# Expert items with the single group first, spread capacities, and recurrence gates between projection tiles

## The chip, the cores and the metric

The kernel runs on one core of one Trainium2 chip. The metric is the device time of the whole program in microseconds. TensorE (PE), VectorE (DVE), ScalarE (ACT), GpSimd (POOL) and SyncE (SP) each run their own instruction stream and meet at semaphores. All data is float32.

## The reference

Two models in a row, on 256 tokens of width 1024. The first block is a mixer of mLSTM and differential attention, followed by a mixture of 32 experts, of which each token takes four:

```python
top_val, top_idx = lax.top_k(logits, TOP_K)          # 4 of 32
gate = jax.nn.softmax(top_val, axis=-1)
hcat = xf[tok] @ w1[e] + b1[e]                       # 1024 -> 2048
act = h_glu * jax.nn.sigmoid(SWIGLU_ALPHA * h_glu) * (h_lin + 1)
y = act @ w2[e] + b2[e]                              # 1024 -> 1024
```

The second block has two layers on 272 tokens (16 of them meta tokens). Its first layer's mixer is a gated linear recurrence beside a sliding-window attention:

```python
r = sigmoid(blockwise(x, w_a) + b_a); i = sigmoid(blockwise(x, w_x) + b_x)
log_a = -LRU_C * r * softplus(-lam);  a = exp(log_a)
u = sqrt(-expm1(2 * log_a)) * (i * x)
h_t = a_t * h_(t-1) + u_t;            y_a = gelu(gate) * h
```

The attention in the first block takes the difference of two softmaxes: `a = p[:, :, 0] - lam * p[:, :, 1]`, of heads of 64 dimensions each.

## The kernel before

Weights stream through SP's queue in units of 1 MB ([128 partitions, 2048 columns]). Outside the expert stage they go through a ring of R = 6 slots; `project` multiplies one unit as two output tiles of 128 columns each, which ACT copies out of two PSUM banks in turn (`out_bank`, `tile_out`).

**The expert stage.** Tokens of an expert are gathered in groups of 32 (`GROUP`). The experts are sorted by load at run time, and place `j` of the order has room for `CAPACITY[j]` groups; a load above its capacity starts a loop behind the stage (`most > 0`). A place's groups are worked in items of at most two groups (`ITEMS`): for an item, PE multiplies the 8 units of the first matrix (`w1_step`, L2137, four column tiles of 32 rows for each group), and in the next round of the loop the 4 units of the second (`w2`, L2154). Between, ACT and DVE turn and activate the hidden values. Each of the 384 units (32 experts with 8 + 4) is loaded once into one of ES = 14 slots (8 spare places of the arena, and the ring), in the fixed order that the list `order` gives: the first matrix of the expert of item n, then the second matrix of that of item n - 1. The load number n (from 14 on) waits for release number n - 14, and releases come only from the last item of an expert (`released`, L758). After every 8 groups PE gathers the next chunk (`gather`, L2091), after every 4 it scatters results (`scatter`, L2106).

**mLSTM and attention.** In `m_rows` (L1945) PE spreads one of 4 gate rows over the partitions. In `d_scores` (L1996) it makes four score tiles of 128 x 512 for a head, two for each of the two maps; map m uses partitions 64 m to 64 m + 63 of q and k. DVE takes maxima and scales, ACT exponentials and copies; `phase` is a barrier of four engines.

**The recurrence.** PE makes the first two x tiles with `pre_unit`, six more and then eight gate tiles with `project`; after each second unit of the gates come four pairs of small matmuls, `lru_gates` (L2316). ACT copies the tiles, takes sigmoids, tanh, exponentials, one square root over everything (L1115), the GELUs, and only then copies K and V (L1123 and L1126), which PE's q tiles (L2343) wait for through the banks. DVE convolves x, computes 1/(1+tanh) and the products (`lru_input`), and after the square root multiplies, scans and multiplies by the gate for each of 8 tiles (`lru_scan`, L1692 to L1696). Then `swa_mask` (L1711) begins the sliding-window attention. POOL only clears two halves of kz here.

## Time and profile before

| | us |
|---|---|
| median of 3 runs | 2896.99 |
| lowest and highest | 2896.99, 2903.4 |
| the profiled execution | 2903.46 |
| its span, first to last instruction | 2901.6 |
| PE busy | 2517.1 (87%) |
| DVE busy | 768.3 (26%) |
| ACT busy | 552.0 (19%) |
| POOL busy | 16.3 (1%) |
| HBM read | 604.91 MB, 209 GB/s over the span |

A busy engine in the table is a mean over stages that have different limits. Lines such as L2137 are those of the kernel before. A timeline row is the start, the time that the group of like instructions takes, the engine, the line, the operation with output and inputs, and in brackets the idle time before it and what ended that.

### The profile page before, as it was taken

Reading aid. Unit: us, or ns where it says so; the run is one execution under the profiler, and the core shown is the slowest. Engines: PE = TensorE matmul, PEld = TensorE weight load, DVE = VectorE, ACT = ScalarE, POOL = GpSimd, SP = SyncE. Lnnn points to the kernel's source line nnn. Section 1 sums busy time; section 2 is a strip of 40 time slices with the busy share of each in tenths; the row PEclk is TensorE's granted clock in tenths of the full one; section 3 lists DMA queues with packets and bytes.
Section 4 is the critical chain, followed back from the end, with each engine's and each line's share of the span. In section 5 each row is a group of like instructions: output and inputs, shape, how many; then the busy total and the mean of one; then the engine's idle time right before and its main releaser. Section 6 shows DMA issues by size and latency. Waiting matters only on the chain. (4 is left out here: it accounts for less than half of the span.)

```text
span 2901.6 us, 36397 instructions
## 1 busy us (share of the span) xinstructions
PE 2517.1 (87%) x15176; PEld 1647.3 (57%) x15176; DVE 768.3 (26%) x1863; ACT 552.0 (19%) x1358; POOL 16.3 (1%) x25
## 2 busy tenths in 40 slices
PE   3999976779899898887868776989999999999998
PEld 1785743468634334332323223767887788667876
DVE  1010046621211111211101112670541325624421
ACT  2110111500212111111111112351211211412110
POOL 0000000000000000000000000000000000100000
PEclk7899997889799999989999897989999999999999
DMA  6222231025276999999999996313333334113432
GB/s 268 70 104 102 101 146 58 0 95 230 87 324 264 421 421 420 420 420 421 421 421 421 421 420 252 121 68 116 116 136 120 131 136 145 44 73 116 145 114 75
DMA packets 88101, 608.35 MB, mean 210 GB/s; under 512 B 10560, under 2 KB 12992, under 8 KB 17248
## 3 DMA queue, kind: packets, MB, share of 16 engines
q1 hardware_dynamic: 84752, 599.82, 52.2%
q10 hardware_dynamic: 3088, 5.78, 0.5%
q8 instruction: 122, 2.00, 0.3%
q0 software_dynamic: 96, 0.39, 0.0%
q14 instruction: 43, 0.35, 0.0%
HBM read 604.91 MB, written 1.05 MB: 209 GB/s over the span
## 5 line engine op out<-in xcount | busy, mean ns | idle before, releaser
L495 PE MATMUL bank<-arena,ring 128*128 128x272 f32 (+2 forms) x3456 | 826.1, 402 | 19.5 <-DVEq L559 18.4
L495 PEld LDWEIGHTS bank<-arena,ring 128*128 128x128 f32 x3456 | 658.9, 191 | 181.8 <-issue 45.9
L2137 PE MATMUL bank<-arena 128*32 128x512 f32 x2304 | 286.9, 620 | 50.1 <-DMA arena<-in_w_e 49.9
L521 PE MATMUL bank<-arena,ring 128*128 128x272 f32 x1216 | 287.7, 396 | 6.1 <-DVE arena L1640 6.1
L521 PEld LDWEIGHTS bank<-arena,ring 128*128 128x128 f32 x1216 | 233.0, 192 | 56.7 <-DVE arena L1640 7.0
L1516 DVE TENSOR_TENSOR arena<-bank,arena 128x256 f32<-128x256 f32 x56 | 23.8, 424 | 841.1 <-PE bank L2116 841.1
L2137 PE MATMUL bank<-ring,arena 128*32 128x512 f32 x1280 | 172.6, 654 | 41.4 <-DMA ring<-in_w_e 41.1
L2137 PEld LDWEIGHTS bank<-arena 128*32 128x32 f32 x2304 | 64.4, 111 | 216.4 <-DMA arena<-in_w_e 109.5
L2154 PE MATMUL bank<-arena 128*32 128x256 f32 x1760 | 118.8, 412 | 43.7 <-DMA arena<-in_w_e 39.7
L1626 DVE SCALAR_TENSOR_TENSOR arena<-arena,par 128x272 f32<-128x272 f32 x296 | 148.5, 502 | 10.5
L2154 PE MATMUL bank<-ring,arena 128*32 128x256 f32 x1824 | 115.0, 398 | 28.8 <-DMA ring<-in_w_e 25.5
L963 ACT ACTIVATE arena<-bank 32x256 f32<-32x256 f32 x224 | 84.0, 375 | 279.3 <-PE bank L2154 276.9
L2154 PEld LDWEIGHTS bank<-arena 128*32 128x32 f32 x1760 | 57.7, 116 | 109.0 <-DMA arena<-in_w_e 51.0
L2137 PEld LDWEIGHTS bank<-ring,arena 128*32 128x32 f32 x1280 | 34.2, 113 | 142.9 <-DMA ring<-in_w_e 93.1
L1624 DVE TENSOR_SCALAR arena<-arena,par 128x272 f32<-128x272 f32 x128 | 53.8, 421 | 215.4 <-ACT arena L1066 161.4
L507 PE MATMUL bank<-ring,arena 128*128 128x256 f32 x512 | 110.8, 379 | 0.0
L2154 PEld LDWEIGHTS bank<-ring,arena 128*32 128x32 f32 x1824 | 60.5, 113 | 88.1 <-DMA ring<-in_w_e 35.2
L507 PEld LDWEIGHTS bank<-ring,arena 128*128 128x128 f32 x512 | 97.3, 190 | 14.1 <-issue 1.0
L555 DVE RECIPROCAL arena<-arena 128x272 f32<-128x272 f32 x8 | 14.8, 1853 | 332.6 <-ACT arena L549 332.6
L977 ACT ACTIVATE arena<-bank 128x512 f32<-128x512 f32 x56 | 33.4, 597 | 287.4 <-PE bank L2137 287.4
L1066 ACT ACTIVATE arena<-bank 128x272 f32<-128x272 f32 x84 | 33.4, 398 | 266.2 <-PE bank L495 266.2
L1307 DVE TENSOR_SCALAR arena<-bank,acol 128x256 f32<-128x256 f32 x32 | 13.2, 477 | 202.8 <-PE bank L1945 202.8
(381 smaller groups left out, 2124.4 us busy)
## 6 DMA issues: line engine op xcount, KB each, us to landing
arena<-in_w_e SPq DMA_DIRECT2D x224, 1024.0 KB, 26.0
ring<-in_w_e SPq DMA_DIRECT2D x160, 1024.0 KB, 26.2
ring<-in_w_up SPq DMA_DIRECT2D x44, 1024.0 KB, 4.8
ring<-in_w_l SPq DMA_DIRECT2D x37, 1024.0 KB, 4.8
ring<-in_w_ada SPq DMA_DIRECT2D x24, 1024.0 KB, 6.2
ring<-in_w_proj SPq DMA_DIRECT2D x24, 1024.0 KB, 4.7
ring<-in_w_down SPq DMA_DIRECT2D x32, 704.0 KB, 4.0
ring<-in_w_merge SPq DMA_DIRECT2D x16, 1024.0 KB, 4.7
```

The source lines that it names most:

```text
L495: mm = pe.matmul(o[:, 0:n], ring[:, s, k * 256 + c * P:k * 256 + (c + 1) * P], rhs(k), start=(k == 0), stop=(k == KT - 1))
L507: mm = pe.matmul(o[:, 0:256], lhs(k, t), ring[:, s, k * 256:(k + 1) * 256], start=(k == 0), stop=(k == KT - 1))
L521: mm = pe.matmul(o[:, 0:n], ring[:, s, k * P:(k + 1) * P], rhs(part * kt + k), start=(part == 0 and k == 0), stop=(part == parts - 1 and k ...
L555: chain(dve.reciprocal(rs, rs))
L963: ins = act.activation(ys[j * GROUP:(j + 1) * GROUP, (g // QUAD) % 2, q * 256:(q + 1) * 256], bank[q * GROUP:(q + 1) * GROUP, 7, i * 256:( ...
L977: act.activation(ht[:, g % 2, :], bank[:, 4 + g % 2, :], ACT.Copy).then_inc(sem("ht_ready"), 1)
L1066: act.activation(up[:, j % 2, c, 2:], o[:, 0:L], ACT.Copy).then_inc(free, 1)
L1516: biased = step(dve.tensor_tensor(four(gate), four(bank[:, 6, 0:256]), bias(0, e), ALU.add))
L1624: chain(dve.tensor_scalar(dst, src[:, 0:L], w(0), b, ALU.mult, ALU.add))
L1626: ins = dve.scalar_tensor_tensor(out=dst, in0=src[:, k:k + L], scalar=w(k), in1=dst, op0=ALU.mult, op1=ALU.add)
L2137: mm = pe.matmul(bank[q * GROUP:(q + 1) * GROUP, 4 + g % 2, :], xe[:, (g // CHUNK) % 2, k, s:s + GROUP], w[:, q * 512:(q + 1) * 512], star ...
L2154: mm = pe.matmul(bank[q * GROUP:(q + 1) * GROUP, 7, i * 256:(i + 1) * 256], actT[:, n % 2, k, i * GROUP:(i + 1) * GROUP], w[:, c * D + q * ...
```

## The change

It does five things.

1. An expert with an odd number of groups starts with the item of one group; the pairs follow.
2. The capacities stay the same numbers in another order.
3. In the mLSTM, `m_rows` takes all 128 partitions of `crow`, which DVE clears ahead. In attention, q is copied by POOL into two tensors `qz`, each with the other map's 64 partitions zero, and the scores multiply all 128 partitions.
4. In the recurrence, the gate matmuls stand behind single tiles of the projections (`behind`); ACT takes the sigmoids there, copies K and V before the square root; DVE's softplus of lambda comes behind the convolutions.
5. The products x * i and gate * h go from DVE to POOL, with the semaphores `lru_gated` and `lru_scanned`.

```diff
-CAPACITY = [3, 1, 5, 1, 1, 4, 1, 1, 4, 1, 1, 3, 1, 3, 1] + [2, 1] * 8 + [1]
+CAPACITY = [3, 1, 2, 1, 3, 1, 2, 1, 4, 1, 2, 1, 1, 5, 1, 1, 2, 1, 4, 1, 2, 1, 3, 1, 2, 1, 2, 1, 1, 2, 1, 1]
...
-    for _g in range(0, _n, 2):
-        ITEMS.append((_at, list(range(STARTS[_at] + _g, STARTS[_at] + min(_g + 2, _n))), _g == 0, _g + 2 >= _n))
+    for _g in range(-(_n % 2), _n, 2):
+        ITEMS.append((_at, list(range(STARTS[_at] + max(_g, 0), STARTS[_at] + _g + 2)), _g <= 0, _g + 2 >= _n))
...
+                    if behind is not None:
+                        behind(2 * unit + c)
...
+        qz = [arena[:, a:a + NH_D * T].rearrange("p (a b) -> p a b", a=NH_D)
+              for a in (vm_at - 4 * 2 * T, vm_at + KT * T)]
...
+                if n >= 3:
+                    lru_sigmoids(n - 3)
+            def gate_tile(n):
+                o, free = tile_out(act, at, n % 2 == 1)
+                act.activation(ga[:, n, :], o[:, 0:L], ACT.Copy).then_inc(free, 1)
+
+            for n in range(3):
+                gate_tile(n)
+                lru_sigmoids(n + 5)
...
-            gate_tiles(2)
+            gate_tile(3)
             act.wait_ge(sem("lru_tanh"), 8)
             for n in range(8):
                 act.activation(rg[:, n, :], rg[:, n, :], ACT.Exp, scale=nlru[:, n:n + 1]).then_inc(sem("lru_decay"), 1)
-            gate_tiles(3)
-            act.wait_ge(sem("lru_ratio"), 8)
-            act.activation(th[:, :, :], th[:, :, :], ACT.Sqrt, scale=2.0).then_inc(sem("lru_root"), 1)
+            for n in range(4, 8):
+                gate_tile(n)
...
             act.activation(v0[0:META, 2, :], o[0:META, 2 * P:3 * P], ACT.Copy).then_inc(free, 1)
+            act.wait_ge(sem("lru_ratio"), 8)
+            act.activation(th[:, :, :], th[:, :, :], ACT.Sqrt, scale=2.0).then_inc(sem("lru_root"), 1)
...
+            chain(dve.memset(crow[:, :, :, :], 0.0))
...
-                dve.wait_ge(sem("xc_ready"), n + 1)
-                chain(dve.tensor_tensor(xc[:, n, :], xc[:, n, :], ig[:, n, :], ALU.mult))
 
             def lru_scan(n):
 
+                dve.wait_ge(sem("lru_gated"), n + 1)
                 chain(dve.tensor_tensor(xc[:, n, :], xc[:, n, :], th[:, n, :], ALU.mult))
-                chain(dve.tensor_tensor_scan(out=ig[:, n, :], data0=rg[:, n, :], data1=xc[:, n, :], initial=0.0,
-                                             op0=ALU.mult, op1=ALU.add))
-                dve.wait_ge(sem("lru_gelu"), n + 1)
-                dve.tensor_tensor(mix[:, n, :], ga[:, n, :], ig[:, n, :], ALU.mult).then_inc(sem("lru_mixed"), 1)
+                dve.tensor_tensor_scan(out=ig[:, n, :], data0=rg[:, n, :], data1=xc[:, n, :], initial=0.0,
+                                       op0=ALU.mult, op1=ALU.add).then_inc(sem("lru_scanned"), 1)
...
+            phase(pool, 1)
+            for m in range(2):
+                pool.memset(qz[m][64 * (1 - m):64 * (2 - m), :, :], 0.0)
+                pool.tensor_copy(qz[m][64 * m:64 * m + 64, :, :], qd[64 * m:64 * m + 64, :, :])
...
+            for n in range(8):
+                pool.wait_ge(sem("xc_ready"), n + 1)
+                pool.wait_ge(sem("lru_gate_read"), n + 1)
+                pool.tensor_tensor(xc[:, n, :], xc[:, n, :], ig[:, n, :], ALU.mult).then_inc(sem("lru_gated"), 1)
+            for n in range(8):
+                pool.wait_ge(sem("lru_scanned"), n + 1)
+                pool.wait_ge(sem("lru_gelu"), n + 1)
+                pool.tensor_tensor(mix[:, n, :], ga[:, n, :], ig[:, n, :], ALU.mult).then_inc(sem("lru_mixed"), 1)
...
-                pe.matmul(bank[:, 2 + i % 2, :], cst("ident", h, 1)[0:4, :].to_broadcast([4, P]), crow[0:4, d, :, :],
+                pe.matmul(bank[:, 2 + i % 2, :], cst("ident", h, 1).to_broadcast([P, P]), crow[:, d, :, :],
...
-                    pe.matmul(bank[:, j, :], qd[64 * m:64 * m + 64, h, qt * P:(qt + 1) * P],
-                              kd[64 * m:64 * m + 64, h, :], start=True, stop=True).then_inc(sem("scores"), 1)
+                    pe.matmul(bank[:, j, :], qz[m][:, h, qt * P:(qt + 1) * P], kd[:, h, :],
+                              start=True, stop=True).then_inc(sem("scores"), 1)
...
-            pre_unit()
-            project(pe, at, 3, ub_k, L, first=ub_first)
-            at.ub += KT
-            pe.wait_ge(sem("lru_loaded"), 16)
...
-            for half in range(2):
-                project(pe, at, 1, ub_k, L)
-                for n in range(4 * half, 4 * half + 4):
-                    lru_gates(n)
-            project(pe, at, 2, ub_k, L)
+            pre_unit()
+            pe.wait_ge(sem("lru_loaded"), 16)
+            project(pe, at, 3, ub_k, L, first=ub_first, behind=lambda c: lru_gates(c - 1) if c >= 1 else None)
+            at.ub += KT
+            project(pe, at, 4, ub_k, L, behind=lambda c: lru_gates(c + 5) if c < 3 else None)
```

## Rows read from the trace of the kernel before

**Rows 1.** GB/s of the page's 40 slices of 72.5 us

```profile
GB/s 268 70 104 102 101 146 58 0 95 230 87 324 264 421 421 420 420 420 421 421 421 421 421 420 252 121 68 116 116 136 120 131 136 145 44 73 116 145 114 75
```

**Rows 2.** windows: us, busy us of each engine, granted clock, DMA share, GB/s

```profile
783.00:815.00 32.00, 31.77 (x203) 16.49 (x206) 1.37 (x7) 4.87 (x7) 0.00 (x0) 0.86 0.03 6
...
877.00:902.00 25.00, 24.16 (x240) 14.56 (x236) 0.62 (x2) 5.80 (x13) 0.00 (x0) 1.00 0.05 7
...
902.00:1772.00 870.00, 710.95 (x6808) 276.37 (x6800) 123.82 (x427) 139.76 (x327) 0.00 (x0) 0.93 1.01 421
```

**Rows 3.** waits of SP's queue, 700 to 910: total us, times, longest

```profile
SPq L758 <- PE bank L2137: 89.6, 18, 37.4
```

**Rows 4.** timeline of PE, one of the paced steps: start, us, [idle before <- releaser]

```profile
1690.36 1.92 PE L2137 MATMUL bank<-arena 128*32 128x512 f32 x16 [0.58 <-DMA arena<-in_w_e]
```

**Rows 5.** timeline of PE, expert stage

```profile
797.96 15.72 PE L2137 MATMUL bank<-arena 128*32 128x512 f32 x144
...
834.59 3.64 PE L2154 MATMUL bank<-ring,arena 128*32 128x256 f32 x64
...
878.08 3.72 PE L2106 MATMUL bank<-arena 128*128 128x256 f32 x16
```

**Rows 6.** timeline of SP's queue, expert stage

```profile
900.09 1.19 SPq L758 DMA_DIRECT2D arena<-in_w_e  x2
```

**Rows 7.** timeline of PE, attention: scores (L1996) and values (L2014)

```profile
545.16 2.07 PE L1996 MATMUL bank<-arena 64*128 64x512 f32 x8
...
550.23 1.99 PE L2014 MATMUL bank<-arena 128*128 128x256 f32 x8 [0.69 <-ACT arena L899]
...
552.15 2.06 PE L1996 MATMUL bank<-arena 64*128 64x512 f32 x8
...
571.19 3.78 PE L2014 MATMUL bank<-arena 128*128 128x256 f32 x8 [0.69 <-ACT arena L899]
```

**Rows 8.** groups by form, PE, 100 to 350: count, busy us, mean ns

```profile
L495 PE MATMUL bank<-arena,ring 128*128 128x512 f32 x192 | 82.8, 593 | 0.0
```

**Rows 9.** timeline of PE, mLSTM: value matmuls

```profile
400.90 3.72 PE L1963 MATMUL bank<-arena 128*128 128x256 f32 x16 [0.92 <-DVE arena L1330]
...
414.14 6.70 PE L1963 MATMUL bank<-arena 128*128 128x256 f32 x16 [4.89 <-DVE small L1330]
```

**Rows 10.** timeline of POOL

```profile
742.87 1.80 POOL L1856 MEMSET arena<- 128x2048 f32 x1 [140.97 <-DVEq L559]
...
2505.03 0.77 POOL L1864 TENSOR_TENSOR arena<-arena 128x272 f32<-128x272 f32 x1 [2.26 <-DVE arena L1820]
```

**Rows 11.** timeline of DVE: around the second barrier, and beside POOL

```profile
483.74 0.42 DVE L1353 TENSOR_TENSOR arena<-arena,small 128x256 f32<-128x256 f32 x1
...
506.14 0.23 DVE L1368 TENSOR_TENSOR lamc<-par 128x1 f32<-128x1 f32 x2
...
2503.97 0.58 DVE L1814 TENSOR_TENSOR arena<-arena 128x416 f32<-128x416 f32 x1
...
2505.37 0.88 DVE L1814 TENSOR_TENSOR arena<-arena 128x416 f32<-128x416 f32 x1
```

**Rows 12.** timeline of all engines, recurrence

```profile
1885.28 2.02 ACT L1115 ACTIVATE arena<-arena 128x2176 f32<-128x2176 f32 x1 [9.15 <-DVE arena L1686]
...
1887.32 1.28 ACT L1119 ACT_TABLE_LOAD   x1
...
1889.50 0.43 DVE L1692 TENSOR_TENSOR arena<-arena 128x272 f32<-128x272 f32 x1
...
1891.09 0.43 DVE L1692 TENSOR_TENSOR arena<-arena 128x272 f32<-128x272 f32 x1
...
1892.10 6.91 PE L2343 MATMUL bank<-arena,ring 128*128 128x272 f32 x16 [8.62 <-ACT arena L1123]
...
1900.61 0.61 DVE L1711 SCALAR_TENSOR_TENSOR arena<-con,bank 128x384 f32<-128x384 f32 x1
...
1904.64 0.49 PE L2369 MATMUL bank<-con,arena 128*128 128x128 f32 x3
```

More of the change, by code:

```diff
@@ L484, in tile_taken, with project @@
             eng.wait_ge(sem(f"bank_read{b}"), n)
-        def project(pe, at, n_units, rhs, n, first=None):
+        def project(pe, at, n_units, rhs, n, first=None, behind=None):
             for unit in range(n_units):
@@ L1081, in _, with lru_sigmoids @@
             act.activation(lru1[:, :], lru1[:, :], ACT.Exp, scale=-1.0).then_inc(sem("lam_exps"), 1)
+            def lru_sigmoids(n):
+                act.wait_ge(sem("lru_gates"), n + 1)
+                b = 2 * (n % 2)
+                act.activation(rg[:, n, :], bank[:, b, 0:L], ACT.Sigmoid, bias=prm("lru_ba", n))
+                act.activation(ig[:, n, :], bank[:, b + 1, 0:L], ACT.Sigmoid, bias=prm("lru_bx", n))\
+                   .then_inc(sem("lru_gate_read"), 1)
             for n in range(8):
@@ L1087, in _ @@
                     act.activation(xr[:, n, 3:], o[:, 0:L], ACT.Copy).then_inc(free, 1)
-            def gate_tiles(unit):
-                for n in (2 * unit, 2 * unit + 1):
-                    o, free = tile_out(act, at, n % 2 == 1)
-                    act.activation(ga[:, n, :], o[:, 0:L], ACT.Copy).then_inc(free, 1)
-            def lru_sigmoids(n):
-                act.wait_ge(sem("lru_gates"), n + 1)
-                b = 2 * (n % 2)
-                act.activation(rg[:, n, :], bank[:, b, 0:L], ACT.Sigmoid, bias=prm("lru_ba", n))
-                act.activation(ig[:, n, :], bank[:, b + 1, 0:L], ACT.Sigmoid, bias=prm("lru_bx", n))\
-                   .then_inc(sem("lru_gate_read"), 1)
-            for unit in range(2):
-                gate_tiles(unit)
-                for n in range(4 * unit, 4 * unit + 4):
-                    lru_sigmoids(n)
+                if n >= 3:
[6 more added lines that the diff above has]
+                lru_sigmoids(n + 5)
             act.wait_ge(sem("lru_gate_read"), 8)
@@ L1679, in _ @@
                 tile_skip(at, n % 2 == 1)
+            dve.wait_ge(sem("lam_exps"), 1)
+            log1p(dve, chain, lru1[:, :], lru3[:, :], nlru[:, :])
+            chain(dve.tensor_scalar(lru2[:, :], prm("lru_lam", 0, 8), -1.0, 0.0, ALU.mult, ALU.max))
+            chain(dve.tensor_tensor(lru2[:, :], lru2[:, :], lru1[:, :], ALU.add))
+            chain(dve.tensor_scalar(lru2[:, :], lru2[:, :], LRU_C, None, ALU.mult))
+            dve.tensor_scalar(nlru[:, :], lru2[:, :], -1.0, None, ALU.mult).then_inc(sem("nlru_ready"), 1)
+            chain(dve.tensor_scalar(nsink[:, :], prm("sinks", 0, HEADS2 + 2), -1.0, None, ALU.mult))
             def lru_input(n):
@@ L1850, in _ @@
         def _(pool):
-            for n in range(1, 5):
+            phase(pool, 1)
+            for m in range(2):
+                pool.memset(qz[m][64 * (1 - m):64 * (2 - m), :, :], 0.0)
+                pool.tensor_copy(qz[m][64 * m:64 * m + 64, :, :], qd[64 * m:64 * m + 64, :, :])
+            for n in range(2, 5):
                 phase(pool, n)
```

12 lines of the change are left out of this document (3 added, 9 removed).

## The prediction, made before the change was run

> **What bounds the kernel now.** I read the page's 40 slices first. From slice 13 on the DMA engines move about 421 GB/s, eleven slices long; before that, in the expert stage's first slices, GB/s falls to 87, 324 and 264 [rows 1]. So the expert stage (some 780 to 1785 us) is paced by weight transfers, once they run. The windows make it exact: from 902 to 1772 us the queue moves 421 GB/s while PE is busy 711 of 870 us, so one 1 MB unit (1.0486 MB) takes 2.49 us, and in two holes, 783 to 815 and 877 to 902, almost nothing moves [rows 2]. The waits of SP's queue name the cause: 89.6 us of waiting on PE's first expert matmuls, that is, for a slot to come free [rows 3]. The holes, some 32 and 25 us, are time that the stage never gets back, since everything behind them is paced by transfers: where PE has a step, it starts it only when its unit lands [rows 4]. Outside this stage PE bounds most of the time; around the recurrence the chain alternates between DVE and ACT.
>
> **Part 1: single group first, capacities spread.** The capacities are the same multiset (56 groups, 39 items, 17 pairs), so neither the 384 units nor PE's matmuls change, and the overflow loop is entered for the same loads. What changes is when slots come free. There are 14 slots. An expert's first slot is released at the first step of its last item, so an expert of 5 groups keeps 12 slots through two whole items.
> First hole: PE starts the expert matmuls at 797.96; 144 instructions of 15.72 us are 18 group-steps (8 each), so 0.87 us per step of one group [rows 5]. Before, the first release needs 8 steps of the pair and one of the single, 17 group-steps, 14.8 us. After, 8 single steps and one pair step, 10 group-steps, 8.7 us. The first hole ends 6.1 us earlier.
> Second hole: with capacities 3, 1, 5 the third expert blocks the slots while PE works through two pairs; the next load is issued only at 900.09 [rows 6]. After, the third has 2 groups and the fourth 1, so no such hole forms there: 25 us saved. The expert of 5 now stands at the 14th place, inside the steady stretch, and there it makes a hole of its own. From the start of its first unit the queue has work for its 8 first-matrix units, the previous expert's 4 second-matrix units, its own 4 and 2 of the next: 18 x 2.49 = 45 us. PE needs, from that unit on: the single item at the transfers' pace, 12 x 2.49 = 30 us (its own matmuls are under that); then a pair's first matrix, 16 x 0.87 = 13.9; two hidden turns and the single's second matrix 3.6 [rows 5]; the first step of the last pair 1.7; about 2.3 from issue to first bytes, read off between 900.09 and 902 [rows 2, 6]. That is 52 us, and 3.7 more if a scatter falls there [rows 5]. So a hole of 7 to 11 us, and about 5 more when its second-matrix slots are held in the same way one item later: 13 in all, taken between 5 and 25. An expert of 4 (two pairs) releases after 30 + 1.7 us, under 45: no hole. The tail ends in experts of 2, 1, 1 as before.
> Sum of part 1: -6.1 - 25 + 13 = **-18 us**.
>
> **Part 2: attention scores and gate rows over all 128 rows.** A score matmul now multiplies 64 live and 64 zero rows. Before, the eight instructions of a head's four scores take 2.07 us [rows 7], while 192 instructions of the same 512 columns over 128 rows cost 431 ns each (82.8 / 192) [rows 8], 3.45 us for eight. So two of the four ran beside each other, one in each half of the array, and that ends: +1.4 us of PE per head. The Trainium skill, TensorE: Matmul & The Clock Gate, Part 3 (packing small matmuls), says that small-K matmuls in distinct row groups run concurrently; the trace agrees, and this edit gives that up. Is it on the path? The head's period is 6.99 us (545.16 to the next scores at 552.15 [rows 7]) and is set by DVE and ACT. PE's own loop becomes 2.0 (values) + 3.45 + 1.05 (turns) + 0.7 (ACT's copy) = 7.2: +0.2 per head, 8 heads, +1.5. Against it, PE is idle less, and its clock fell in this stage: the same eight value matmuls take 1.99 us at 2.4 GHz and 3.78 at 1.2 GHz after idling [rows 7]. I take 0 for attention, +2 to -4 as bounds at a high clock. The gate rows (4 live rows, now 128) keep their time; in the mLSTM loop the 16 value matmuls take 3.72 us, and 6.70 where PE had idled 4.89 us [rows 9]. Three such places give back at most 6.6 us if fuller matmuls held the clock; the idle time that precedes them stays, so I take -1. The added clears and copies of q stand on POOL between two barriers. A clear of 2048 columns takes 1.80 us; POOL's multiply of 272 columns takes 0.77 [rows 10], so a copy of 2048 is under 5.8: at most 15.2 us together, and DVE needs from its last step before the barrier (484.2) to 506.4 in that place [rows 11]. Hidden; if a copy cost over 9 us it would show. One DVE clear more in the gate stage stands beside projections: 0.
>
> **Part 3: recurrence.** Three moves. (a) The gate matmuls go between projection tiles, so PE doesn't wait for ACT's sigmoids (about 1 us). (b) ACT copies K and V out before the square root. Before, PE idles 8.62 us to 1892.10 for that copy, then runs a q tile in 6.91 us, at 1.2 GHz [rows 12]. That idle goes. But what is late next is DVE: its mask at 1900.61 waits for the scans, and those for the root. The root (2.02, plus a table load of 1.28) now stands behind the V copy; V ends at 1892.10 - 8.62 = 1883.5, about 1.4 less with (a), so the root ends at 1886 instead of 1887.3. (c) DVE's scan loop gives the second multiply to POOL. A period is 1.59 us before [rows 12] and 1.16 without the 0.43 of a multiply; over 8, -3.4. However both engines then read two operands from SBUF at once. The row bears on that: a DVE multiply of 416 columns takes 0.58 us alone and 0.88 while POOL's multiply (0.77) runs [rows 10, 11]. With POOL's 0.77 falling between each DVE multiply and scan, I put a period at 1.75, between 1.16 and 1.16 + 0.77, and the loop at 1.3 us longer than before. The Trainium skill, SBUF — State Buffer, "Who interferes with whom", calls the shared port an exclusive lock, held for the whole instruction, against a DVE instruction with two SBUF inputs; by it the period would be 1.93, and the 0.88 agrees in kind. So the mask comes at 1900.4, where it was. And PE, which before had just run a q tile when the first probabilities came (1904.64 [rows 12]), has by then done two q tiles and idled some 10 us, after which I expect 1.2 GHz: its q tile of 6.91 us shows some 7 us of such work, in which 3.5 are lost, now inside the PE-bound loop of 6.6 us. Part 3: **+3 us** (-5 if ports don't collide and the clock holds; +4). POOL's first multiplies wait for gates that are long read; nothing that is queued behind them is due before the next phase.
>
> **Sum.** -18 + 0 - 1 + 3 = -16 us. The profiled execution took 2903.5 us (span 2901.6 and 1.9 around it), the median of three runs is 2897.0, 6.5 lower. I carry the difference over: 2897 - 16 = **2881 us**. About 0.3%, 8.7 us, is what a measurement of this kernel can tell from no change.
>
> **Rivals.**
> A, no hole at the expert of 5: if PE is far enough ahead there, all of 31 us is won, 2868. Against it is that PE cannot be ahead of the transfers.
> B, the hole is as large as before: 25, and -6 remains: 2893, within 0.3%. For it: the same 12 slots, the same two further items.
> C, the fuller matmuls hold TensorE's clock in mLSTM and attention: another -8: 2873. For it, both places fall after idle time; against, the idle time before the mLSTM ones isn't touched.
> D, ports don't collide and the clock survives in part 3: -5 in place of +3: 2873.
> E, slower: the array stays at 1.2 GHz through attention, where the scores are now serial. A head would be 3.8 (values) + 6.9 + 2.0 + 0.7 = 13.4 against 7.2 on average, over seven heads +43: 2881 + 43 = 2924. It decides from the point where PE's loop at the low clock exceeds DVE's 7 us. Against it: PE would then be busy 95% of the time, and at 545 and 550 us a less busy PE ran at 2.4 GHz [rows 7].
> F, that the change doesn't do what it says (a capacity that a load exceeds) would start the overflow loop; the sorted capacities are the same, so I give it nothing.
>
> **How the numbers follow.** Chances: forecast 0.48, A 0.09, B 0.13, C 0.13, D 0.12, E 0.05. Forecast, A, C and D are faster by over 8.7 us: 0.82 and, with the edge of B, 0.84; within 0.3%: 0.12; slower: 0.04. The range leaves out E and the far ends of A and B: 2864 to 2893.
>
> **What would show it.** Right: in the windows after the change, transfers resume near 809, run without a hole past 900, and pause 8 to 15 us near 1200; the last expert's work ends 18 us earlier. The score group takes about 3.5 us a head, head periods stay near 7. PE's q tile follows V's tile at once, and the mask starts within 2 us of where it does, counted from the start of the projections. Wrong: a hole at 870 to 900 that stays, head periods over 8 us, or POOL's copies ending after DVE's part of that phase.

## The result

The changed kernel takes 2872.64 us (median of 4 runs, 2872.32 to 2876.0) against 2897.26 us (2896.99 to 2903.4): a ratio of 0.9913, with a 95% interval of 0.9895 to 0.993. The prediction was 2881 us in a range of 2864 to 2893. The sign and the largest term were right, and the gain was 8 us larger than forecast. Two of the smaller terms were wrong, as the sections below show. The 2872.64 us lie at the 2873 us of the rivals C and D and not at the forecast.

The span of the profiled execution is 2870.6 us, against 2901.6 before. Windows of the expert stage after; columns as in [rows 2]:

```profile
783.00:811.00 28.00, 28.00 (x226) 11.78 (x228) 2.01 (x6) 5.28 (x8) 0.00 (x0) 0.96 0.40 152
811.00:1170.00 359.00, 307.35 (x2993) 124.04 (x2986) 54.86 (x190) 61.94 (x145) 0.00 (x0) 0.92 1.01 418
1170.00:1230.00 60.00, 58.81 (x613) 25.98 (x615) 8.83 (x30) 12.56 (x29) 0.00 (x0) 1.00 0.78 310
```

The run of transfers now reaches from 811 to 1170 us at 418 GB/s; the gap of 877 to 902 us [rows 2] is gone, and one smaller gap stands at 1170 to 1230, where 310 GB/s instead of 421 are 60 x (1 - 310/421) = 15.8 us lost. SP's issues there show why; two units are issued at 1181.45, and then none for 20 us:

```profile
1181.45 1.50 SPq L763 DMA_DIRECT2D arena<-in_w_e  x2
1202.04 2.05 SPq L763 DMA_DIRECT2D ring<-in_w_e  x2
...
1210.86 2.05 SPq L763 DMA_DIRECT2D ring<-in_w_e  x2
1218.09 2.05 SPq L763 DMA_DIRECT2D arena<-in_w_e  x2
```

**Where the gain is.** To see what belongs to an edit and what to an execution, I took the time between fixed instructions in every profiled execution; each row of this table is such a stretch in us.

| stretch | before | after | after, second execution | same code elsewhere |
|---|---|---|---|---|
| mLSTM: first row sums (L1966, L1983) to the 28 sums behind the loop (L1974, L1991) | 101.35 | 98.46 | 97.92 | 97.9 to 98.5 with the change, 100.7 to 101.4 without |
| the lambda matmul (L1988, L2005) to the first merge matmul (L495) | 93.96 | 90.39 | 90.34 | 90.4 with, 93.0 and 94.0 without |
| expert stage: first expert matmul to DVE's residual add (L1587, L1594) | 990.60 | 974.31 | 974.92 | 974.2 to 975.7 with, 990.5 without |
| recurrence: first projection (L495) to the out-projection (L521, L523) | 148.57 | 144.66 | 145.74 | 143.6 to 145.7 with, 148.4 without |
| merge to the first expert matmul | 197.48 | 196.12 | 196.08 | 195.6 to 197.5, in both codes |
| residual add to the first projection | 25.45 | 23.09 | 25.38 | 23.0 to 25.5, in both codes |
| start to the first row sums | 363.33 | 362.96 | 360.76 | 361.0 to 363.2, in both codes |
| the 28 sums to the lambda matmul | 41.83 | 41.60 | 41.52 | 41.5 to 41.6 with, 41.8 and 40.2 without |
| out-projection to the end | 939.05 | 939.04 | 938.47 | 937.0 to 941.1, in both codes |

In the first four stretches every execution with the change in question is shorter than every one without it: -16.3 (part 1), -2.9 and -3.6 (part 2), -3.9 (part 3), together -26.7 us between these two profiles. The experiments below, which undo one part at a time, give 16.2, 4.9 and 3.8 us for the same stretches. Part 2 is the least certain: without it the 28 sums to the lambda matmul took 40.2 us once, 1.4 less than with it, so that from the first row sums to the merge it is worth 3.5 us by that experiment and 6.7 by the comparison of before and after. The merge and the norm stretch, 3.7 us of the 31.0 between the two spans, change with the execution, and so do the start and the end. The medians give -24.6 in the first comparison and -26.3 in the second (2871.63 against 2897.89).

### The profile page after: what moved, and what is told of

Its sections match the earlier page's. It is cut to its first block and busy times, and to the rows that moved or that the text cites. A ratio compares the mean times of both kernels' runs of the same rounds, so it can differ in the third digit from the quotient of the medians.

```text
span 2870.6 us, 36400 instructions
## 1 busy us (share of the span) xinstructions
PE 2506.2 (87%) x15176; PEld 1645.5 (57%) x15176; DVE 766.7 (27%) x1846; ACT 550.9 (19%) x1358; POOL 36.5 (1%) x45
## 5 line engine op out<-in xcount | busy, mean ns | idle before, releaser
L495 PE MATMUL bank<-arena,ring 128*128 128x272 f32 (+2 forms) x3456 | 827.0, 402 | 19.5 <-DVEq L561 18.4
L495 PEld LDWEIGHTS bank<-arena,ring 128*128 128x128 f32 x3456 | 658.7, 191 | 181.8 <-issue 46.0
L2154 PE MATMUL bank<-arena 128*32 128x512 f32 x2112 | 271.2, 636 | 50.6 <-DMA arena<-in_w_e 50.6
L523 PE MATMUL bank<-arena,ring 128*128 128x272 f32 x1216 | 287.7, 396 | 6.1 <-DVE arena L1647 6.1
L523 PEld LDWEIGHTS bank<-arena,ring 128*128 128x128 f32 x1216 | 233.0, 192 | 56.7 <-DVE arena L1647 7.0
L2154 PE MATMUL bank<-ring,arena 128*32 128x512 f32 x1472 | 187.9, 628 | 49.5 <-DMA ring<-in_w_e 49.5
L2171 PE MATMUL bank<-arena 128*32 128x256 f32 x1984 | 127.4, 402 | 26.9 <-DMA arena<-in_w_e 24.2
L2154 PEld LDWEIGHTS bank<-ring,arena 128*32 128x32 f32 x1472 | 40.2, 111 | 158.3 <-DMA ring<-in_w_e 93.9
L2171 PE MATMUL bank<-ring,arena 128*32 128x256 f32 x1600 | 103.3, 406 | 20.7 <-DMA ring<-in_w_e 16.0
L2171 PEld LDWEIGHTS bank<-ring,arena 128*32 128x32 f32 x1600 | 53.0, 115 | 74.4 <-issue 25.5
L1071 ACT ACTIVATE arena<-bank 128x272 f32<-128x272 f32 x84 | 33.4, 397 | 266.3 <-PE bank L495 266.3
L1057 ACT ACTIVATE arena<-bank 128x272 f32<-128x272 f32 x32 | 12.7, 397 | 282.6 <-PE bank L523 282.6
```

The source lines that it names most:

```text
L495: mm = pe.matmul(o[:, 0:n], ring[:, s, k * 256 + c * P:k * 256 + (c + 1) * P], rhs(k), start=(k == 0), stop=(k == KT - 1))
L523: mm = pe.matmul(o[:, 0:n], ring[:, s, k * P:(k + 1) * P], rhs(part * kt + k), start=(part == 0 and k == 0), stop=(part == parts - 1 and k ...
L1071: act.activation(up[:, j % 2, c, 2:], o[:, 0:L], ACT.Copy).then_inc(free, 1)
L2154: mm = pe.matmul(bank[q * GROUP:(q + 1) * GROUP, 4 + g % 2, :], xe[:, (g // CHUNK) % 2, k, s:s + GROUP], w[:, q * 512:(q + 1) * 512], star ...
L2171: mm = pe.matmul(bank[q * GROUP:(q + 1) * GROUP, 7, i * 256:(i + 1) * 256], actT[:, n % 2, k, i * GROUP:(i + 1) * GROUP], w[:, c * D + q * ...
```

## The experiments

In all of them the times of before were taken on the same chip: 2897.55 us for the first four, 2895.18 for the next four, 2897.89 for the last three. A median of four runs scatters by some 3 us, so for terms of a few us I go by the stretches.

### Part 1 undone

```diff
-CAPACITY = [3, 1, 2, 1, 3, 1, 2, 1, 4, 1, 2, 1, 1, 5, 1, 1, 2, 1, 4, 1, 2, 1, 3, 1, 2, 1, 2, 1, 1, 2, 1, 1]
+CAPACITY = [3, 1, 5, 1, 1, 4, 1, 1, 4, 1, 1, 3, 1, 3, 1] + [2, 1] * 8 + [1]
...
-    for _g in range(-(_n % 2), _n, 2):
...
+    for _g in range(0, _n, 2):
...
```

> The changed kernel with part 1 undone: old capacities, pairs first; parts 2 and 3 stay. Theory (slots held until an expert's last item): in the two traces the expert stage, from the first expert transfer to the end of its last step, takes 17.6 us less after the change, so this one gives 2872.6 + 17.6 = 2890 us, first release about 14.8 us after the first expert matmul, and the pause of the transfers of some 25 us before the third expert's slots come free is back. Rival (the stage gained because of what the other parts do to TensorE's clock): the pause is back but the time stays under 2880.

Measured: 2886.8 us, ratio 0.9954 (0.9937 to 0.9971). The expert stage takes 990.52 us, as before the change (990.60); the first release comes 15.06 us after the first expert matmul (9.06 with the change), and by windows of 5 us some 27.7 us of transfers are lost between 860 and 895 us. So part 1 is worth 16.2 us of this stretch and needs no help from the others; the medians differ by 14.2. The 17.6 that I expected contained 1.3 us from ahead of the first expert matmul, which is a matter of the execution.

### Single first alone, in the kernel before

```diff
-    for _g in range(0, _n, 2):
-        ITEMS.append((_at, list(range(STARTS[_at] + _g, STARTS[_at] + min(_g + 2, _n))), _g == 0, _g + 2 >= _n))
+    for _g in range(-(_n % 2), _n, 2):
+        ITEMS.append((_at, list(range(STARTS[_at] + max(_g, 0), STARTS[_at] + _g + 2)), _g <= 0, _g + 2 >= _n))
```

> The kernel before with nothing but the single group first; old capacities (3, 1, 5, ...). Theory: the second pause ends when the last item of the expert of 5 begins. Ahead of that step PE now has 7 groups of the first matrix and 5 of the second instead of 8 and 6, at 6.9 and 3.6 us a group, less 0.9 because the step itself is of a pair: the pause ends 9.7 us earlier, and the 6.1 us of the first pause are inside that, not on top. 2897.3 - 9.7 = 2887.6 us. Rival 1 (the two pauses are separate sums, only the first shrinks): -6.1, 2891. Rival 2 (the order within an expert doesn't matter): 2897.

Measured: 2893.15 us, ratio 0.9976 (0.9964 to 0.9989); the expert stage 986.39 us, 4.2 less than before. The interval of the time, -3.2 to -10.4 us, holds both rival 1's -6.1 and my -9.7 and decides nothing; the stage says that it was less than either. SP's issues from the end of the second pause, in this kernel and behind it in the kernel before:

```profile
891.90 2.05 SPq L758 DMA_DIRECT2D arena<-in_w_e  x2
896.07 2.05 SPq L758 DMA_DIRECT2D ring<-in_w_e  x2
900.23 5.48 SPq L758 DMA_DIRECT2D arena<-in_w_e  x4
913.14 1.22 SPq L758 DMA_DIRECT2D ring<-in_w_e  x2
```

```profile
902.54 1.19 SPq L758 DMA_DIRECT2D ring<-in_w_e  x2
904.98 2.91 SPq L758 DMA_DIRECT2D arena<-in_w_e  x4
915.32 1.22 SPq L758 DMA_DIRECT2D ring<-in_w_e  x2
```

Counted from the first expert matmul (797.41 and 797.96), the pause ends after 94.5 us instead of 102.1, 7.6 us earlier, which is near the 9.7 of the account. But then the last item is a pair: a slot comes free every 2.1 us, as each step has two groups' work (two units each at 891.90, 896.07, 900.23), where before one came free in 1.2 (two from 900.09 [rows 6], two from 902.54, four from 904.98). The next slots, of the expert behind it, come at 913.14, 115.7 us after the first matmul, against 915.32 and 117.4: 1.6 us earlier. By then PE has multiplied all five groups by the first matrix, in either order. So the order within an expert sets when its first slots come; what comes behind them is set by the whole expert's work, and 4.2 us remain at the end of the stage. My account had stopped at the first release.

### Pairs first, in the changed kernel

```diff
-    for _g in range(-(_n % 2), _n, 2):
-        ITEMS.append((_at, list(range(STARTS[_at] + max(_g, 0), STARTS[_at] + _g + 2)), _g <= 0, _g + 2 >= _n))
+    for _g in range(0, _n, 2):
+        ITEMS.append((_at, list(range(STARTS[_at] + _g, STARTS[_at] + min(_g + 2, _n))), _g == 0, _g + 2 >= _n))
```

> The changed kernel with its new capacities, but pairs first as before. Theory: the first release comes 6.1 us later, and at the expert of 5 a pair's second matrix (7.1 us) stands ahead of the release instead of a single's (3.6), with a single's step (0.9) instead of a pair's (1.7): 2.7 us more pause there, perhaps twice. 2872.6 + 6.1 + 2.7 to 5.4 = 2881 to 2884 us. Rival (all of part 1's gain is that the expert of 5 stands later): 2873.

Measured: 2873.93 us, ratio 0.9909 (0.9892 to 0.9926), which by the times alone can't be told from the changed kernel's. The expert stage is 977.76 us, 3.45 more. The first release is 6.0 us later (15.07 after the first matmul), as the account says. The pause at the expert of 5 got shorter, not longer: from 1165 to 1225 us the mean is 327 GB/s, 60 x (1 - 327/421) = 13.4 us lost instead of 15.8:

```profile
1165.00:1225.00 60.00, 54.25 (x598) 22.15 (x598) 9.68 (x32) 9.52 (x22) 0.00 (x0) 0.97 0.80 327
```

The reason lies in the same point. PE can't be ahead of the transfers, so the expert's first item runs at their pace; with a pair there, three groups are left behind it instead of four. So 12.8 of the 16.2 us of part 1 (990.52 to 977.76) are the new order of the capacities; the order within an expert brings 3.5, which is 6.0 at the start less 2.4 here.

### The expert of 5 as pair, single, pair

```diff
-    for _g in range(-(_n % 2), _n, 2):
-        ITEMS.append((_at, list(range(STARTS[_at] + max(_g, 0), STARTS[_at] + _g + 2)), _g <= 0, _g + 2 >= _n))
+    _split = {5: [2, 1, 2]}.get(_n, [1] * (_n % 2) + [2] * (_n // 2))
+    for _i, _w in enumerate(_split):
+        _g = STARTS[_at] + sum(_split[:_i])
+        ITEMS.append((_at, list(range(_g, _g + _w)), _i == 0, _i == len(_split) - 1))
```

> The changed kernel, the expert of 5 groups worked as pair, single, pair instead of single, pair, pair. Its first item runs at the pace of the transfers (30 us for 12 units) whether it has one group or two (a pair needs 21 us), so the larger one should be there. Theory: ahead of the release stand a single's first matrix (6.9 instead of 13.9) and a pair's second (7.1 instead of 3.6): 3.4 us less pause at the first matrix and about as much or more at the second, since one group less (10.5 us) is left behind the first item. 2872.6 - 3.4 to -10 = 2863 to 2869 us, and a pause near 1200 us that is shorter by as much. Rival (the pause is set by all five groups' work): 2872.6.

Measured: 2867.14 us, ratio 0.9891 (0.9874 to 0.9907); the expert stage 970.32 us, 4.0 less.

```profile
1165.00:1225.00 60.00, 54.09 (x574) 21.66 (x570) 11.18 (x37) 11.43 (x27) 0.00 (x0) 0.97 0.85 340
```

60 x (1 - 340/421) = 11.5 us are lost at the pause instead of 15.8. The single group first pays at the very start, where everything is loaded and PE is late (6.0 us); at the expert of 5, inside the paced stretch, the larger item belongs first. For the experts of 3 this was not tried by itself.

### Part 2 undone

```diff
-                pe.matmul(bank[:, 2 + i % 2, :], cst("ident", h, 1).to_broadcast([P, P]), crow[:, d, :, :],
+                pe.matmul(bank[:, 2 + i % 2, :], cst("ident", h, 1)[0:4, :].to_broadcast([4, P]), crow[0:4, d, :, :],
...
-                    pe.matmul(bank[:, j, :], qz[m][:, h, qt * P:(qt + 1) * P], kd[:, h, :],
-                              start=True, stop=True).then_inc(sem("scores"), 1)
+                    pe.matmul(bank[:, j, :], qd[64 * m:64 * m + 64, h, qt * P:(qt + 1) * P],
+                              kd[64 * m:64 * m + 64, h, :], start=True, stop=True).then_inc(sem("scores"), 1)
```

(and the clears and copies left out)

> The changed kernel with part 2 undone: gate rows from 4 partitions, scores from 64, no clears and copies of q. Theory of the forecast: mLSTM + 1, attention 0: 2873.6 us; score groups 2.07 us again, head period 6.99. Theory from the trace after (fuller matmuls held the clock): mLSTM's end came 3.3 us earlier after the change and attention's last values another 1.3: 2872.6 + 4.8 = 2877.4 us, with some heads at 1.2 GHz (values 3.78 us) before the last. Rival (which heads run at 1.2 GHz differs from execution to execution whatever the matmuls): 2873, low heads or not.

Measured: 2874.65 us, ratio 0.9931 (0.9915 to 0.9948). The median, 2.0 us above the changed kernel's, hardly speaks. The stretches: mLSTM 100.72 us (98.46 with the change, 101.35 before), lambda matmul to merge 93.02 (90.39, 93.96), but between these two 40.2 (41.6, 41.8). Timeline rows of PE at these places, in this kernel and then in the changed one:

```profile
363.97 1.12 PE L1957 MATMUL bank<-arena,con 4*128 4x512 f32 x2
...
384.91 5.15 PE L1975 MATMUL bank<-arena 128*128 128x256 f32 x16 [4.89 <-DVE small L1336]
...
412.73 6.58 PE L1975 MATMUL bank<-arena 128*128 128x256 f32 x16 [4.89 <-DVE small L1336]
...
483.90 5.15 PE L1991 MATMUL bank<-arena,con 128*128 128x256 f32 x16 [3.57 <-ACT arena L539]
...
517.96 3.47 PE L2026 MATMUL bank<-arena 128*128 128x256 f32 x8 [0.69 <-ACT arena L904]
...
572.42 5.26 PE L2032 MATMUL bank<-arena,con 128*128 128x256 f32 x16 [1.15 <-ACT arena L539]
```

```profile
364.68 1.02 PE L1962 MATMUL bank<-arena,con 128*128 128x512 f32 x2
...
385.34 5.38 PE L1980 MATMUL bank<-arena 128*128 128x256 f32 x16 [4.89 <-DVE small L1337]
...
413.01 5.38 PE L1980 MATMUL bank<-arena 128*128 128x256 f32 x16 [4.89 <-DVE small L1337]
...
482.45 6.52 PE L1996 MATMUL bank<-arena,con 128*128 128x256 f32 x16 [3.57 <-ACT arena L539]
...
516.68 1.99 PE L2031 MATMUL bank<-arena 128*128 128x256 f32 x8 [0.69 <-ACT arena L904]
518.51 3.60 PE L2013 MATMUL bank<-arena 128*128 128x512 f32 x8
...
525.55 3.60 PE L2013 MATMUL bank<-arena 128*128 128x512 f32 x8
...
571.29 3.69 PE L2037 MATMUL bank<-arena,con 128*128 128x256 f32 x16 [1.15 <-ACT arena L539]
```

Two things are in the mLSTM's stretch. Two gate rows take 1.02 us over 128 rows and 1.12 over 4. With the matmuls just ahead of them, which end 0.1 us sooner as well, that is 0.19 us a time and 1.1 us over the six times in the stretch. The rest is TensorE's clock. Three groups of 16 value matmuls stand behind 4.89 us of idle time; 3.72 us is what such a group takes at 2.4 GHz throughout (at 400.90 [rows 9]). They took:

| | first | second | third |
|---|---|---|---|
| without full rows, 3 executions | 5.15 to 5.37 | 6.58 to 6.70 | 5.38 to 5.68 |
| with full rows, 10 executions | 5.24 to 5.38 | 5.12 to 5.38 | 5.07 to 5.29 |

Only the second differs by over a microsecond in each of them, and at the next place it goes the other way: the 16 sums behind 3.57 us of idle time take 5.15 us in this kernel, 6.43 to 6.55 with full rows, and 6.74 in the kernel before. So behind the same idle time the same matmuls came out short in one place and long in another, in either kernel. That full rows bring the clock back sooner in the mLSTM is not shown; where a group falls in time is a rival that stands.

In attention the sign is the same in all of them. The first values take 1.99 us in all ten executions with full scores and 3.47 to 3.78 in the three without, the 16 sums at the end 3.69 against 5.26 to 5.92, and the stretch to the merge 90.3 to 90.4 against 93.0 to 94.0. The granted clock agrees: 0.82 and 1.00 from 505 to 515 and 515 to 525 us in the changed kernel, 0.50 and 0.70 in this one. Whether the reason is the rows themselves, the longer busy time of the scores (3.60 us against 2.06) or, again, where the stage falls in time was not tried.

### Part 3 undone

The changed kernel with the recurrence of the kernel before (items 4 and 5 of the change backwards); its core:

```diff
-            project(pe, at, 3, ub_k, L, first=ub_first, behind=lambda c: lru_gates(c - 1) if c >= 1 else None)
+            project(pe, at, 3, ub_k, L, first=ub_first)
...
+            for half in range(2):
+                project(pe, at, 1, ub_k, L)
+                for n in range(4 * half, 4 * half + 4):
+                    lru_gates(n)
```

> The changed kernel with part 3 undone: gate matmuls in two blocks, root ahead of the K and V copies, all products on DVE; parts 1 and 2 stay. Forecast: part 3 costs 3 us, so 2869.6. Theory from the trace after: from the first projection matmul of the recurrence to the steady q tiles it gained 2.0 us, so 2874.6. Rival: two more differences belong to it, 2.4 us less in the norm ahead of the projections and 1.8 us less behind the last q tile, both at 1.2 GHz in the trace before: 2878.8. If those were chance, they show here in any case or in none.

Measured: 2875.79 us, ratio 0.9929 (0.9912 to 0.9946). From the first projection to the out-projection 148.45 us (144.66 with the change). So part 3 gains 3.8 us where I had put a loss of 3; against the second execution of the changed kernel (145.74) it is 2.7. The two other differences that I named are not part 3's: the norm's 25.4 us came back in the second execution of the changed kernel.

### The gate product back on DVE

```diff
-                dve.tensor_tensor_scan(out=ig[:, n, :], data0=rg[:, n, :], data1=xc[:, n, :], initial=0.0,
-                                       op0=ALU.mult, op1=ALU.add).then_inc(sem("lru_scanned"), 1)
+                chain(dve.tensor_tensor_scan(out=ig[:, n, :], data0=rg[:, n, :], data1=xc[:, n, :], initial=0.0,
+                                             op0=ALU.mult, op1=ALU.add))
+                dve.wait_ge(sem("lru_gelu"), n + 1)
+                dve.tensor_tensor(mix[:, n, :], ga[:, n, :], ig[:, n, :], ALU.mult).then_inc(sem("lru_mixed"), 1)
```

> The changed kernel with the product gate * h back on DVE (x * i stays on POOL). Theory: DVE and POOL share their way to SBUF; a scan takes 1.17 us beside POOL's product and 0.72 alone. Here the scans are 0.72 again, the period is 0.44 + 0.72 + 0.43 = 1.59 instead of 1.53, and the mask starts 0.5 us later: 2873. Rival (the scan took 1.17 for another reason): scans of 1.17 and a period of 1.96, 3.4 us later: 2876.

Measured: 2876.0 us, ratio 0.9928 (0.9912 to 0.9945). One period, here and in the changed kernel (DVE, then POOL):

```profile
1863.84 0.43 DVE L1698 TENSOR_TENSOR arena<-arena 128x272 f32<-128x272 f32 x1
1864.31 0.72 DVE L1699 TENSOR_TENSOR_SCAN arena<-arena 128x272 f32<-128x272 f32 x1
...
1865.43 0.43 DVE L1698 TENSOR_TENSOR arena<-arena 128x272 f32<-128x272 f32 x1
```

```profile
1859.91 0.42 DVE L1698 TENSOR_TENSOR arena<-arena 128x272 f32<-128x272 f32 x1
1860.37 1.17 DVE L1699 TENSOR_TENSOR_SCAN arena<-arena 128x272 f32<-128x272 f32 x1
1861.45 0.41 DVE L1698 TENSOR_TENSOR arena<-arena 128x272 f32<-128x272 f32 x1
...
1860.08 0.87 POOL L1877 TENSOR_TENSOR arena<-arena 128x272 f32<-128x272 f32 x1 [30.82 <-DVE arena L1699]
1861.61 0.87 POOL L1877 TENSOR_TENSOR arena<-arena 128x272 f32<-128x272 f32 x1 [0.66 <-DVE arena L1699]
```

The scan is 0.72 us again and the period 1.59, against 1.17 and 1.53. From the first scan to the mask it is 12.22 us against 11.37: 0.85 more, 0.5 for the eight periods and 0.4 for the last product, which on POOL nobody waits for. The profiled execution was the slowest of the four, and the rest of its 6.9 us over the changed kernel's lies where the code is the same: the norm took 24.66 us (23.09), the matmuls ahead of the experts 1.3 more, and the part behind the recurrence 1.9 more. The medians differ by 3.4 us; that those are such differences too is not shown.

### The root ahead of the K and V copies

```diff
+            act.wait_ge(sem("lru_ratio"), 8)
+            act.activation(th[:, :, :], th[:, :, :], ACT.Sqrt, scale=2.0).then_inc(sem("lru_root"), 1)
             act.wait_ge(sem("bank_read0"), at.out // 2)
...
             act.activation(v0[0:META, 2, :], o[0:META, 2 * P:3 * P], ACT.Copy).then_inc(free, 1)
-            act.wait_ge(sem("lru_ratio"), 8)
-            act.activation(th[:, :, :], th[:, :, :], ACT.Sqrt, scale=2.0).then_inc(sem("lru_root"), 1)
```

> The changed kernel with the square root back ahead of the GELUs and of the K and V copies; the rest of part 3 stays. Theory: the start of the attention is set by DVE's mask, which waits for the scans, which wait for the root. DVE's last ratio is ready at 1849.8, so the root ends near 1852 instead of 1858.8, scans end near 1864, and the mask starts 6.6 us earlier than in the changed kernel, at 1864: 2866. V is copied near 1857, so the first q tile comes 2 us later and is hidden. Rival (PE's idle time ahead of its first q tile sets it to 1.2 GHz as before the change, which eats 3.5 us): 2869.5. Rival 2 (K and V copies are what mattered): 2875.

Measured: 2865.61 us, ratio 0.9899 (0.9883 to 0.9916). ACT's root, DVE's first product and mask, and PE's first q tile and first turn:

```profile
1849.39 2.02 ACT L1121 ACTIVATE arena<-arena 128x2176 f32<-128x2176 f32 x1 [2.32 <-DVE arena L1693]
...
1851.44 0.44 DVE L1698 TENSOR_TENSOR arena<-arena 128x272 f32<-128x272 f32 x1 [2.08 <-ACT arena L1121]
...
1863.39 0.58 DVE L1715 SCALAR_TENSOR_TENSOR arena<-con,bank 128x384 f32<-128x384 f32 x1
...
1856.21 3.90 PE L2356 MATMUL bank<-arena,ring 128*128 128x272 f32 x16 [1.79 <-ACT arena L1129]
...
1867.21 0.55 PE L2382 MATMUL bank<-con,arena 128*128 128x128 f32 x3 [1.30 <-DVE arena L1733]
```

From the first projection to the mask it is 76.9 us, against 83.7 in the changed kernel: 6.8 us, all of it kept to the end (7.0 by the medians). V is copied at 1856.09. PE's idle time ahead of the q tile is 1.79 us, and the tile takes 3.90 us, at 2.4 GHz, so the first rival is out; ahead of the first turn 1.30 us are left of 9.93. So part 3 without this one move would gain 10.7 us instead of 3.9. The mask, as the prediction said, is what is late, and moving the root behind the copies held it back.

### The changed kernel again, and two better ones

The changed kernel once more; the changed kernel with both edits of above (pair, single, pair and the early root); and the same with the root in two instructions:

```diff
+            for n, (a, z) in enumerate(((0, 6), (6, 8))):
+                act.wait_ge(sem("lru_ratio"), z)
+                act.activation(th[:, a:z, :], th[:, a:z, :], ACT.Sqrt, scale=2.0).then_inc(sem("lru_root"), 1)
...
-            dve.wait_ge(sem("lru_root"), 1)
...
             for n in range(8):
+                dve.wait_ge(sem("lru_root"), 1 if n < 6 else 2)
                 lru_scan(n)
```

> The changed kernel once more, to see which stretches of two executions of the same code differ. Theory: the stretches that gained beyond their instructions in the first comparison (from the end of the expert stage to the first projection 25.5 to 23.1 us, from the first expert transfer to the first expert matmul 98.1 to 96.8) belong to executions and not to the edits: here they may show either value, while the expert stage from first to last step (974.3), the stretch from the step between the mixers to the merge (90.4) and the one from the first projection of the recurrence to the mask (83.7) come out within 0.3 us. Median 2872. Rival (they are effects of the edits): 23.1 and 96.8 again.

> The changed kernel with both improvements: the expert of 5 worked as pair, single, pair, and the square root ahead of the GELUs and the K and V copies. Theory: the two stand in different stages and add up: 4.0 us of the expert stage and 6.8 of the recurrence, by the two traces. 2872 - 10.8 = 2861 us. Rival (part of the gain of either was chance of its executions): 2865 to 2868.

> The same with the square root in two instructions, tiles 0 to 5 and 6 to 7, so that the first part runs beside DVE's last two ratios. Theory: the scans start when DVE's ratios end (2.1 us earlier than with one root), the mask would follow 2.1 us earlier, but it needs PE's first scores, which end about 0.7 us after that point: mask 1.4 us earlier, 2859.6 us. Rival (PE's q tile, due after the V copy, is now what is late, and a shorter idle time doesn't count): the same time as with one root, 2861.

Measured: 2871.63 us (0.9908, 0.9891 to 0.9924), 2861.31 (0.9873, 0.9857 to 0.989) and 2858.51 (0.9867, 0.9851 to 0.9884). The second execution of the changed kernel shows what differs without an edit: its norm stretch is 25.38 us, as before the change, with the same code as the one that took 23.09. The stretch from the first expert transfer to the first expert matmul stayed low here (96.8 us), but was 98.1 in the kernel with the gate product on DVE, whose code there is the changed kernel's. The stages of the change repeated, the expert stage to 0.6 us, not to 0.3. Both edits add up (10.3 us of the 10.8). With the root in two, the first projection to the mask takes 74.8 us instead of 76.9: the whole 2.1, not 1.4, since V's copy and so the scores come 1.4 us earlier too. How DVE's and POOL's products meet shows here too (DVE's products and scans from the first on, then POOL's):

```profile
1844.33 0.43 DVE L1701 TENSOR_TENSOR arena<-arena 128x272 f32<-128x272 f32 x1
1844.80 0.73 DVE L1702 TENSOR_TENSOR_SCAN arena<-arena 128x272 f32<-128x272 f32 x1
1845.44 0.42 DVE L1701 TENSOR_TENSOR arena<-arena 128x272 f32<-128x272 f32 x1
...
1847.62 0.94 DVE L1701 TENSOR_TENSOR arena<-arena 128x272 f32<-128x272 f32 x1
1848.60 1.17 DVE L1702 TENSOR_TENSOR_SCAN arena<-arena 128x272 f32<-128x272 f32 x1
1849.69 0.93 DVE L1701 TENSOR_TENSOR arena<-arena 128x272 f32<-128x272 f32 x1
...
1846.98 4.25 POOL L1880 TENSOR_TENSOR arena<-arena 128x272 f32<-128x272 f32 x4 [23.12 <-ACT arena L1128]
```

While POOL has no product, because the GELUs aren't there, a period is 1.09 us (1845.44 to 1846.53); once it catches up on four products in a row, DVE's multiply takes 0.94, its scan 1.17 and a period 2.07 (1847.62 to 1849.69).

## Why the prediction was right, and where it wasn't

**Part 1, -18 predicted, -16.3 measured.** The first hole: 6.1 us predicted, 6.0 measured (15.06 to 9.06 us from the first expert matmul to the first release). The second hole of 25 us (27.1 by windows of 5 us) is gone. The hole at the expert of 5: 7 to 11 and about 5 behind it were worked out and 13 taken; by windows of 5 us, 10.8 are lost from 1190 to 1210 and 5.0 behind that, 15.8 in all. The 3.7 us for a scatter, priced and left out of the sum, fell there too: PE's scatter at 1212.31 (3.72 us) stands between SP's issues at 1210.86 and 1218.09. A place that the sum lacked, gathers and a scatter near 1030 us, lost 2.3. So rival A (no hole) and rival B (as large as before) are out. The reason given was right for the first-matrix slots, but the prediction held the single group first to be a gain everywhere, and at this expert it costs 4.0 us against a pair, since the first item's work is hidden whatever it is.

**Part 2, attention 0 predicted, -3.6 measured (-2.6 by the experiment); mLSTM -1, -2.9 measured (-2.3).** The instructions came out as costed: scores 3.60 us (3.45), a head's period 7.04 (7.2), POOL's copies 1.88 and 1.89 us (under 5.8) and hidden from 481.0 to 488.4. By the Trainium skill, TensorE: Matmul & The Clock Gate, Part 3 (packing small matmuls), small matmuls in different row groups run at the same time, which this edit gives up; the 2.06 and 3.60 us agree with it. The stage got shorter all the same. Two steps failed. One is "The gate rows (4 live rows, now 128) keep their time": they take 1.02 us instead of 1.12, and that is 1.1 of the mLSTM's 2.9 us. The other is the 0 for attention and the -1 for the clock in the mLSTM, "the idle time that precedes them stays, so I take -1". The idle time did stay (4.89 us); of the three places one is unchanged (5.37 and 5.38 us), one went from 6.70 to 5.38 and one from 5.68 to 5.24, 1.8 us in all. These 1.8 are near the -1 and, by the sums behind the loop, need not be the edit's; the 0 for attention is the larger miss. Rival C named a clock that is held, with 8 us more for it; from the first row sums to the merge the two profiles give 5.7 more than the -1, the experiment 2.5 more. The bounds (+2 to -4, and 6.6 at most) held both. Rival E (1.2 GHz through attention) is out: from 516.68 us on all values take 1.99 until the last. Why attention's clock was higher stays open.

**Part 3, +3 predicted, -3.9 measured (-2.8 with the second execution of the changed kernel).** This is the step with the wrong sign. Timeline rows of the changed kernel, ACT's V copy and root, DVE's first product and mask, and PE from the first q tile on:

```profile
1854.91 0.38 ACT L1130 ACTIVATE arena<-bank 128x256 f32<-128x256 f32 x1 [3.97 <-PE bank L2346]
...
1856.75 2.02 ACT L1133 ACTIVATE arena<-arena 128x2176 f32<-128x2176 f32 x1
...
1858.80 0.44 DVE L1698 TENSOR_TENSOR arena<-arena 128x272 f32<-128x272 f32 x1 [8.99 <-ACT arena L1133]
...
1870.64 0.58 DVE L1715 SCALAR_TENSOR_TENSOR arena<-con,bank 128x384 f32<-128x384 f32 x1
...
1854.80 3.93 PE L2356 MATMUL bank<-arena,ring 128*128 128x272 f32 x16
...
1874.45 0.90 PE L2382 MATMUL bank<-con,arena 128*128 128x128 f32 x3 [9.93 <-DVE arena L1733]
1875.15 1.65 PE L2370 MATMUL bank<-arena 128*128 128x128 f32 x4
1876.59 0.85 PE L2382 MATMUL bank<-con,arena 128*128 128x128 f32 x3
1877.23 0.91 PE L2370 MATMUL bank<-arena 128*128 128x128 f32 x4
1877.97 3.83 PE L2356 MATMUL bank<-arena,ring 128*128 128x272 f32 x16
```

Taken in order. The V copy and q tile come at once, as said. The root ends 71.8 us after the first projection, before 73.3 (1887.30 [rows 12] less 1814.01): 1.5 earlier, 1.3 predicted. The scans take 11.8 us, 1.53 a period, where 1.75 was predicted: that is 1.8 us. The estimate between 1.16 and 1.93 leaned on the 0.88 of a multiply beside POOL [rows 10, 11]; in fact only the scan is held up, by 0.45, and the multiply ahead of it runs beside POOL's product at 0.41. By the Trainium skill, SBUF — State Buffer, "Who interferes with whom", the port that VectorE and GpSimd share is an exclusive lock. The scan agrees: it ends 0.6 us behind POOL's product, about its own length alone. The period of 1.93 that I took from it doesn't come, because I counted POOL's product as behind the multiply: the multiply starts first, at 1861.45 against POOL's 1861.61, and isn't delayed. Where POOL's products stand back to back, in the kernel with two roots, both are delayed and the period is 2.07. The last product of 0.4 is off the path too, which the sum forgot. Then PE: it idled 9.93 us, as predicted (10), and was at 1.2 GHz behind it, as predicted (granted clock 0.50 from 1874 to 1877 us). But the low rows (0.90, 1.65 and 0.85 us) end at 1877.23, 2.8 us on; the next scores (0.91) and the q tile (3.83) are at 2.4 GHz (0.97 from 1877 to 1885). I had put 7 us of such work and 3.5 lost, from the one q tile of 6.91 [rows 12]. From the mask to the first steady q tile (1913.73 before, 1884.61 after) it is 13.12 before and 13.97 after: 0.85 lost. So the mask was put 2.7 us too late and the clock's loss 2.7 too high; what is left, up to 1.9 us behind the steady q tiles, differs between executions of the changed code (from the mask to the out-projection 59.9 to 62.0 us; 61.8 to 62.0 with the old recurrence). Rival D had the sign (-5), but neither of its conditions held as stated: the clock fell, for 2.8 us only, and DVE's scan did meet POOL's product.

**The sum.** By the two profiles the errors are 5.5 us in part 2 and 6.9 in part 3, both in one direction, and part 1 was put 1.7 too high: the four stretches give 26.7 us where 16 were predicted. By the experiments, with part 2 at its 3.5 us, it is 23.5. The time lay in the range because the range was wide enough for rivals C and D: the bounds of the unknown costs (-4 in attention, -6.6 in the mLSTM loop, -5 in the recurrence) reached as far as the errors did. C and D together had been given 0.25, and the forecast's own sums for parts 2 and 3 did not hold; that the errors stayed inside the range is in part luck.

## What to carry to other kernels

When buffers are released only at an item's end and transfers set the pace, try the largest work unit first in a group, since it runs under the transfers (4.0 us here, for one group of five), and the smallest first where everything is already loaded and the compute engine is late. Before moving a copy ahead of an operation on ACT, ask which of the two the last-arriving engine waits for: here the early copies only gave PE 10 us of idle time, and the early root gave the whole kernel 6.8 us. And compare several executions by stretches between fixed instructions before explaining a difference of 3 us: several stretches here differed by 1.3 to 2.4 us between executions of the same code, and the long one at the end by 4.

## What was unexpected of the hardware

- In attention TensorE was at 2.4 GHz earlier with scores over all 128 rows, slower in themselves (3.60 us against 2.06): the first values took 1.99 us in ten executions of ten, and 3.47 to 3.78 in three of three without. In the mLSTM the same 16 matmuls behind the same 4.89 us of idle time took between 5.07 and 6.70 us, in one and the same execution 5.37, 6.70 and 5.68.
- Two matmuls of 512 columns over 128 rows, between others over 128 rows, took 1.02 us; over 4 rows 1.12.
- A DVE multiply of 272 columns beside a POOL multiply took 0.41 us where it started 0.16 us ahead of it, no longer than alone, and the scan behind it 1.17 instead of 0.72; with POOL's products back to back both were longer, 0.94 and 1.17.
- POOL copies 64 x 2048 in 1.88 us, as long as it clears them (1.80).
- After 9.93 us of idle time TensorE was at 1.2 GHz for 2.8 us of work only; before the change, after 8.62 us, for most of a q tile of 6.91 (granted clock 0.56 from 1892 to 1899 us).
